# Prompt tile routed ahead of the other tiles' output projection, modulation rows by DMA, output weights read during the attention

## The reference

```python
def trunk_layer(x, cvec, p, layer, ctx, rope):
    sh1, sc1, gt1, sh2, sc2, gt2 = modulation(cvec, p['w_mod'], p['b_mod'])   # silu(c) @ w_mod + b_mod, split in 6
    h = rms_norm(x, p['g_norm1']) * (1 + sc1) + sh1
    mix, ctx_out = token_mixers(h, p, layer, ctx, rope)      # three attentions, concatenated, then @ w_out
    x = x + gt1 * mix
    h = rms_norm(x, p['g_norm2']) * (1 + sc2) + sh2
    x = x + gt2 * peer_ffn(h, p['w_pq'], p['peer_keys'], p['peer_u'], p['peer_v'])
    return x, ctx_out

def peer_ffn(h, w_pq, peer_keys, peer_u, peer_v):            # 8 heads, 128 x 128 experts, 16 chosen per head
    q = (t @ w_pq).reshape(n, PEER_HEADS, 2, PEER_DQ // 2)
    sub = jnp.einsum('nhpd,hpkd->nhpk', q, peer_keys)
    sc, ix = lax.top_k(sub, PEER_TOPK)
    cand = sc[:, :, 0, :, None] + sc[:, :, 1, None, :]       # 256 candidates a head
    best, pos = lax.top_k(cand, PEER_TOPK)
    experts = jnp.take_along_axis(cand_ix, pos, axis=-1)
    gates = softmax(best)
    act = gelu(einsum('nd,nhkd->nhk', t, peer_u[experts]))   # one gathered row of 1024 per token and expert
    return einsum('nhk,nhkd->nd', gates * act, peer_v[experts])
```

## Time and profile before

| | us |
|---|---|
| median of 3 runs | 5324.46 (5318.93 to 5358.44) |
| the profiled execution | 5334.77 |
| its span, first to last instruction | 5333.0 |

### The profile page before, as it was taken

How to read it: one execution, slowest core, us unless ns; L and a number is a source line. 1 busy time by engine, 2 the same in 40 slices (tenths; PEclk the granted TensorE clock), 3 DMA queues, 4 the chain that set the end, 5 groups by cost and what they waited for, 6 DMA issues and landing times. The chain is left out here.

```text
span 5333.0 us, 51151 instructions
## 1 busy us (share of the span) xinstructions
PE 4446.2 (83%) x15092; PEld 2252.2 (42%) x15092; DVE 3367.1 (63%) x8542; ACT 1394.3 (26%) x3530; POOL 2773.5 (52%) x2690
## 2 busy tenths in 40 slices
PE   7999898788878878777699998987988788887775
PEld 4588664333323323222256885643333233332222
DVE  5556564666676666766465655646666666766664
ACT  1211452222222222222212125422222222222221
POOL 0122000677777777777601220007777777777775
PEclk9988899899999999999999988899999999999999
DMA  7000001999999999999970000029999999999998
GB/s 263 27 3 1 16 1 68 363 409 409 409 399 406 408 404 397 400 401 397 355 251 1 3 1 16 1 96 399 409 409 409 401 401 406 400 401 393 401 390 314
DMA packets 425564, 1471.61 MB, mean 276 GB/s; under 512 B 46528, under 2 KB 52288, under 8 KB 424768
## 3 DMA queue, kind: packets, MB, share of 16 engines
q0 software_dynamic: 368640, 1342.34, 63.8%
q1 hardware_dynamic: 56640, 125.89, 6.6%
HBM read 1464.49 MB, written 3.57 MB: 275 GB/s over the span
## 5 line engine op out<-in xcount | busy, mean ns | idle before, releaser
L1601 PE MATMUL psall<-ring,diag 128*128 128x512 f32 x5120 | 2482.8, 614 | 672.2 <-DMA ring<-in_peer_v,eidx 554.0
L1413 DVE CUSTOM_DVE_ANT_0 ring<-ring,mixed 128x1024 f32<-128x1024 f32 x1280 | 1565.5, 1223 | 1010.3 <-DMA ring<-in_peer_u,eidx 1010.2
L1332 POOL DMA_INDIRECT ring<-in_peer_u,eidx x1280 | 1294.5, 1011 | 1152.4 <-DVE eidx L1270 762.4
L1601 PEld LDWEIGHTS psall<-ring,diag 128*128 128x128 f32 x5120 | 889.1, 190 | 2221.5 <-DMA ring<-in_peer_v,eidx 1468.4
L1332 POOL DMA_INDIRECT ring<-in_peer_v,eidx x1280 | 1303.8, 1019 | 408.3 <-issue 261.9
L1498 ACT ACTIVATE act<-dot 128x2 f32<-128x2 f32 x640 | 130.1, 203 | 2265.4 <-DVE dot L1413 2265.4
L1490 ACT ACTIVATE diag<-cons,wgt 128x128 f32<-128x128 f32 x1280 | 443.0, 393 | 209.6 <-DVE wgt L1393 207.6
L493 POOL TENSOR_TENSOR mlt<-lt,lmask 128x512 f32<-128x512 f32 x120 | 173.1, 1452 | 518.5 <-DVE lt L591 359.6
L1557 PE MATMUL psall<-h2T,wq 128*128 128x128 f32 (+1 forms) x1024 | 285.6, 434 | 1.3 <-DVE x L1375 1.3
L1557 PEld LDWEIGHTS psall<-h2T,wq 128*128 128x128 f32 x1024 | 157.3, 191 | 132.0 <-issue 130.2
L485 POOL MEMSET state<- 64x512 f32 x2 | 1.0, 518 | 392.2 <-POOLq L396 392.2
(11 more groups left out here) (291 smaller groups left out, 4918.8 us busy)
## 6 DMA issues: line engine op xcount, KB each, us to landing
wlate<-in_w_mod SPq DMA_DIRECT2D x32, 1024.0 KB, 5.3
wq<-in_w_pq SPq DMA_DIRECT2D x64, 512.0 KB, 6.8
ring<-in_peer_u,eidx POOLq DMA_INDIRECT x1280, 10.5
ring<-in_peer_v,eidx POOLq DMA_INDIRECT x1280, 10.5
w<-in_w_mod SPq DMA_DIRECT2D x4, 2048.0 KB, 11.2
wtm<-in_w_mod SPq DMA_DIRECT2D x4, 2048.0 KB, 18.6
wtm<-in_w_in_tm SPq DMA_DIRECT2D x4, 2048.0 KB, 9.6
ring<-in_w_out SPq DMA_DIRECT2D x4, 2048.0 KB, 11.2
```

The costliest lines, as they stand in the source:

```text
L1332: nc.gpsimd.indirect_dma_start(out=ring[:, n % slots, :], out_offset=None, in_=d[table], in_offset=bass.IndirectOffsetOnAxis(ap=p.eidx[:, ...
L1413: nc.vector.tensor_tensor_reduce(out=p.u[:, n % UR, :], in0=p.u[:, n % UR, :], in1=p.mixed[:, t, :], scale=1.0, scalar=0.0, op0=ALU.mult, ...
L1601: mm = nc.tensor.matmul(bank, p.diag[:, n % VR, :], p.v[:, n % VR, 512 * c:512 * c + 512], start=(s == 0), stop=(s == UNIT - 1))
```

## The change

- **Modulation.** The bias rows are loaded (`bias`) and added in the first step of each late chunk's sum. The sum over partitions becomes one product for each conditioning vector that leaves a row of 512 in one partition; ScalarE copies it to `mrow` and, after each pair, issues a store of the two rows to a DRAM tensor `mid_rows`. It waits for the store before its next late copy, and for all eight at the block's end. The final two steps on VectorE go.
- **Preparation.** The 22 copies of keys and values move from ScalarE to VectorE.
- **Attention.** The output weights are issued on SP's queue at the attention's start, into `u`, the tile of the u slots, which is now a tile of its own that stands from there on.
- **Tail.** The spreads go. Seven broadcasts (`gt1` x 2, `sc2` x 2, `g_norm2`, `sh2` x 2) are issued on SP's queue ahead of the keys; two more (`gt2`) after the eighth query weight. VectorE forms `(1 + sc2) * g_norm2` first. TensorE turns the prompt's h2 and makes its first queries and scores after two tiles' projections; VectorE does the steps of head 0's routing between the other tiles' residuals and norms. GpSimd waits for `h2_ready` of all tiles before the first gather of `peer_v` only.

```diff
@@ mod_and_project, SP, at each late chunk's first half
+                            sp.wait_ge(sem("bias_zero"), 1)
+                            sp.dma_start(p.bias[0:1, i % 2, :], d["b_late"][bass.ds(lay, 1), i]).then_inc(sem(f"load_bias{i % 2}"), 16)
@@ ScalarE
+                if kind == "late" and i >= 1 and a == 0:
+                    act.wait_ge(sem("row_store"), 16 * i)
                 dst, src = proj_evac(p, j, kind, i, a, b)
                 nc.scalar.activation(dst, src, ACT.Copy).then_inc(sem("proj_out"), 1)
+                if kind == "late" and a == 1:
+                    act.wait_ge(sem("proj_out"), j + 1)
+                    nc.scalar.dma_start(d["mid_rows"][i // 2:i // 2 + 1, :, WCH * (i % 2):WCH * (i % 2) + WCH],
+                                        p.mrow[0:1, :, :]).then_inc(sem("row_store"), 16)
+            act.wait_ge(sem("row_store"), 16 * LATE)
@@ VectorE
-                            late.mark(nc.vector.tensor_scalar(acc, w_late[:, k, :], p.sc[:, k, g:g + 1], None, ALU.mult))
+                            late.mark(nc.vector.scalar_tensor_tensor(out=acc, in0=w_late[:, k, :], scalar=p.sc[:, k, g:g + 1],
+                                                                     in1=p.bias[:, i % 2, :], op0=ALU.mult, op1=ALU.add))
...
@@ TensorE
-                    for blk in range(4):
-                        for g in range(2):
-                            last = nc.tensor.matmul(bank[:, 2 * blk + g:2 * blk + g + 1], sums_late[:, i % 3, g, blk * P:(blk + 1) * P],
-                                                    p.ones[:, 0:1], start=True, stop=True)
-                    last.then_inc(sem("proj"), 1)
+                    nc.tensor.matmul(bank[0:1, :], p.ones[:, 0:1], sums_late[:, i % 3, a, :], start=True, stop=True).then_inc(sem("proj"), 1)
...
@@ attend
+        @block.sync
+        def _(sp):
+            for c in range(2):
+                sp.dma_start(p.wout[:, c, :, :], d["w_out"][bass.ds(lay, 1), :, :, WCH * c:WCH * c + WCH].rearrange("l p k n -> p (l k) n")
+                             ).then_inc(sem(f"load_wout{c}"), 16)
@@ tail, SP
+            for g in range(2):
+                spread(sp, p.rows[:, 0, g, :], d["mid_rows"][0][g:g + 1, :], "load_gt1")
+            for g in range(2):
+                spread(sp, p.rows[:, 1, g, :], d["mid_rows"][2][g:g + 1, :], "load_sc2")
+            spread(sp, p.g2row, d["g_norm2"][bass.ds(lay, 1)], "load_sc2")
+            for g in range(2):
+                spread(sp, p.rows[:, 2, g, :], d["mid_rows"][1][g:g + 1, :], "load_sh2")
@@ GpSimd
             pool.wait_ge(sem("wout_mm"), 2 * NT)
-            pool.wait_ge(sem("h2_ready"), NT)
...
+                    if m == 0:
+                        pool.wait_ge(sem("h2_ready"), NT)
@@ VectorE
+            residual(0)
+            norm(0)
+            residual(1)
+            norm(1)
+            top.mark(nc.vector.memset(p.r_gs[:, :], 0.0))
+            pieces(0, 0, 6)
+            residual(2)
+            pieces(0, 6, 10)
+            norm(2)
+            residual(3)
+            pieces(0, 10, 14)
+            norm(3)
+            residual(4)
+            pieces(0, 14, TOPK)
+            norm(4)
             dve.wait_ge(sem("h2_ready"), NT)
...
+            pieces(1, 0, TOPK)
@@ ScalarE
             square(0)
+            turned(0)
             square(1)
...
+            for j in early[0:5]:
                 evacuate(j)
+            square(2)
+            square(3)
+            top_gates(p, act, 0)
+            square(4)
+            turned(1)
+            for j in early[5:9]:
                 evacuate(j)
+            turned(2)
+            evacuate(early[9])
+            turned(3)
+            turned(4)
+            top_gates(p, act, 1)
@@ TensorE
             project(0)
             project(1)
+            turn(0)
+            for j in early[0:5]:
+                step(j)
             for t in range(2, NT):
                 project(t)
+            turn(1)
             pe.wait_ge(sem("res1"), 2 * NT)
+            for j in early[5:9]:
                 step(j)
+            turn(2)
+            step(early[9])
+            turn(3)
+            turn(4)
```

More of the change, by code:

```diff
@@ L173, in mod_and_project @@
             if blk >= 1:
-                jobs.append(("late", None, blk - 1, 0, 0))
+                jobs += [("late", None, blk - 1, g, 0) for g in range(2)]
     for t in range(NT):
@@ L177, in mod_and_project @@
         if t % 2 == 0:
-            jobs.append(("late", None, 5 + t // 2, 0, 0))
+            jobs += [("late", None, 5 + t // 2, g, 0) for g in range(2)]
     jobs_until = {job[1]: j + 1 for j, job in enumerate(jobs)}
@@ L848, in prepare_attention, with copied @@
     at = {job: j for j, job in enumerate(jobs)}
+    on_vector = [job[0] in ("kn", "v") for job in jobs]
+    def copied(eng, j):
+        if on_vector[j]:
+            eng.wait_ge(sem("p_evd"), sum(on_vector[:j + 1]))
+        else:
+            eng.wait_ge(sem("p_ev"), j + 1 - sum(on_vector[:j + 1]))
     with nc.Block() as block:
@@ L918, in _ @@
                                                accum_out=p.lam[:, i:i + 1]).then_inc(sem("lam_dot"), 1)
+            for j, (kind, t, half) in enumerate(jobs):
+                if not on_vector[j]:
+                    continue
+                dve.wait_ge(sem("p_mm"), j + 1)
+                b = ps[j % 8]
+                if kind == "kn":
+                    lo, hi = (0, 512) if half == 0 else (512, KEYS)
+                    nc.vector.tensor_copy(p.kTb[0:64, t, lo:hi], b[0:64, 0:hi - lo]).then_inc(sem("p_evd"), 1)
+                else:
+                    nc.vector.tensor_copy(p.vb[:, t, :], b[:, :]).then_inc(sem("p_evd"), 1)
             for t in range(1, NT):
-                dve.wait_ge(sem("p_ev"), at[("uq", t, 1)] + 1)
+                copied(dve, at[("uq", t, 1)])
                 x = p.qb[:, t % 2, :].rearrange("p (h c) -> p h c", c=96)[:, :, 64:96]
@@ L1290, in tail, with spread @@
     nc, d, sem, ps = p.nc, p.d, p.sem, p.ps
-    vecs = [p.mod[:, 16:24, :], p.A2[:, :, :], p.mod[:, 24:32, :], p.mod[:, 40:48, :]]
-    spreads = [(v, g, half) for v in range(4) for g in range(2) for half in range(2)]
     steps, before_row = routing_steps()
-    def row_of(v, g):
-        return p.gt2[:, g, :] if v == 3 else p.rows[:, v, g, :]
+    def spread(sp, tile, row, done):
+        sp.dma_start(tile, row.to_broadcast([P, D])).then_inc(sem(done), 16)
     def block_of(g, c, b):
@@ L1321, in _ @@
                              ).then_inc(sem(f"load_q{i % WR}"), 16)
+                if i == 7:
+                    for g in range(2):
+                        spread(sp, p.gt2[:, g, :], d["mid_rows"][3][g:g + 1, :], "load_gt2")
             for name in p.front_sems:
@@ L1366, in norm, with residual @@
                 nc.vector.tensor_tensor(p.mixed[:, t, :], p.mixed[:, t, :], p.rows[:, 2, g, :], ALU.add).then_inc(sem("h2_ready"), 1)
-            for t in range(NT):
+            def residual(t):
                 g = 0 if t == 0 else 1
@@ L1431, in _ @@
                                      ps[t % 2].rearrange("p (k n) -> p k n", k=4), ACT.Copy).then_inc(sem("m_out"), 1)
-            for u, (v, g, half) in enumerate(spreads):
-                act.wait_ge(sem("row_mm"), u + 1)
-                nc.scalar.activation(row_of(v, g)[:, half * 512:half * 512 + 512], ps[2 + u % 2], ACT.Copy).then_inc(sem("row_out"), 1)
             def square(t):
@@ L1492, in _ @@
             j = len(early)
-            act.wait_ge(sem("row_mm"), len(spreads))
             for q in range(ROWS // 2):
@@ L1516, in _ @@
                 last.then_inc(sem("m_turned"), 1)
-            for u in range(len(spreads)):
-                pe.wait_ge(sem("diag2"), u + 1)
-                if u >= 2:
-                    pe.wait_ge(sem("row_out"), u - 1)
-                nc.tensor.matmul(ps[2 + u % 2][:, :], p.ones, p.diag4[:, u % 2, :], start=True, stop=True).then_inc(sem("row_mm"), 1)
             pe.wait_ge(sem("m_out"), NT)
```

122 lines of the change are left out of this document (51 added, 71 removed).

## The result

The changed kernel took 5289.15 us (median of 8 runs, 5285.57 to 5307.93) against 5329.06 us before (median of 8, 5318.93 to 5358.44): ratio 0.9923, 95% interval 0.9907 to 0.994, a gain of 32 to 50 us. The profiled execution took 5288.71 us, its span 5286.9, which is 46.1 less than the 5333.0 of before.

A forecast was written before the change was run, and what follows sets the result against it. DMA transfers bound the expert loop, which could only begin earlier: 24.9 less 3.1 less 2.1 is 19.7 us a layer, 39.4 for two, giving 5295.4 from the profiled 5334.77, scaled by 0.9981 to 5285 us; range 5264 to 5308.

The forecast's parts named there:

- Timeline of the tail: Attention's end to first gather: step times in the new order, first gather at 89.5 us against 114.4, 24.9 earlier per layer.
- Spreads and early weights: Tail's start: spreads' 14.7 us of TensorE go, broadcasts stay hidden, early read keeps output weights from being uncovered.
- First dot: Expert loop's start: first dot on a gathered row about 104 us after the stage's start, 19.1 earlier than 123.1.
- That the first gather carries its 24.9 us into the loop: Loop's start: twelve gathers last 16 us until the first dot, so nothing is lost; upper bound of loss 5.8 us.
- the rival of the first dot: Loop's start: the first dot, not the first gather, starts the loop; gain 13.9 us a layer, 5297 us; chance 0.12.
- Modulation: Modulation stage: added bias steps cost 3.1 us and the store at its end 2.1 us more per layer.
- six times 0.52: Modulation stage: VectorE's two-tensor first steps cost 0.52 us in each of six chunks, 3.1 us a layer.
- the lower bound: Modulation stage: only the sixth chunk's own two steps cost, 0.5 us, the rest absorbed by waits for transfers.
- The store's term: Modulation stage's end: copy, row store and wait for its landing cost 2.1 us more than before; bound 4.8.
- Preparation: Preparation of the attention: 22 copies moved from ScalarE to VectorE stay under TensorE; nothing gained, nothing lost.
- TensorE's clock: Tail's projection: without the spreads it runs at 1.2 GHz; throughout, 69 us more and 5422 us; chance 0.04.
- the rival in which little is lost in modulation: Modulation and loop start: little lost, loop fills faster; gain 23.3 us a layer, 5278 us; chance 0.11.

The follow-up runs named there:

- e1: Changed kernel with the tail's old order again (all five tiles projected before the prompt's queries, scores and routing): 5310.76 us, ratio 0.9955.
- e2: Changed kernel with the output weights' early read undone, issued at the tail's start ahead of the broadcast rows: 5301.62 us, ratio 0.9942.
- e8: Changed kernel with the seven broadcast rows issued behind the routing keys and first four query weights: 5294.01 us, ratio 0.9927.
- e9: Changed kernel with query weights 4 to 7 in other tiles, so 8 to 11 are read behind the prompt's first queries: 5284.31 us, ratio 0.9906.
- e6: Changed kernel with head 1's routing moved from ahead of the first dot to behind the first eight dots: 5283.36 us, ratio 0.9917.
- e3: Changed kernel without the late modulation chunks' bias: rows not loaded, first step one-tensor again; another choice of experts: 5276.94 us.
- e5: Changed kernel with GpSimd's wait for all normed rows back before the first gather, instead of before the second table's: 5293.21 us, ratio 0.993.
- e10: Changed kernel with the late modulation bias added by GpSimd to the copied row, each row stored one chunk later: 5281.6 us, ratio 0.99.
- e11: Changed kernel with query weights ahead, bias on GpSimd, head 1's routing among first dots, last two routing steps before last residual: 5291.27 us, ratio 0.9915.

## Why the prediction was right, and where it was not

The forecast of 5285 us lay 4 us under the median, its gain (39.4 for the profiled execution) at the measured 39.9; the profiled execution itself gained 46.1. The steps one by one:

- **Timeline of the tail: right to the half microsecond.** Forecast and measured (first layer, from 840.66): first product 5.0 and 4.9; turning the prompt's h2 32.5 and 32.5; queries done 42.1 and 42.2; projections done 84.8 and 85.0; row numbers done 88.5 and 88.4; first gather 89.5 and 89.3.
- **Spreads and early weights: right.** e1 confirms the split, e2 that the weights would have been uncovered (by 4.3 us), e8 that the broadcasts are hidden.
- **First dot: 104 forecast, 103.1 measured.** ScalarE's table loads stood where expected, each at the 1.28 us of the earlier trace rows:

```profile
928.28 1.28 ACT L1493 ACT_TABLE_LOAD   x1
```

- **That the first gather carries its 24.9 us into the loop: nearly.** 25.0 and 25.8 at the first gather, 23.1 and 22.5 at the 200th. The reason given (twelve gathers last until the dot) held: in the first layer no gather waits for the dot, in the second the ninth row buffer is waited for 0.67 us (0.30 is the issue). But it was too simple. It took the loop to be short of transfers from its start on, where for some 32 us GpSimd's issuing sets the pace (e9). And it missed a transfer that the earlier gather collides with: 2 MB of query weights that used to land before it. They cost some 2 us at the 200th gather and not 5.1, because they filled a sag that the old start had. e9 shows this; the rival of the first dot would have given 20 at the 200th gather, which e6 speaks against as well.
- **Modulation: wrong.** Forecast 5.2 us a layer, measured 1.5 (mean of 14 stages against the two of before; 0.9 and 1.4 in the profile shown). The failing step is "six times 0.52", which lies above the middle of its bounds because "the chunks run back to back for VectorE most of the time". They don't: VectorE waited 10.6 us for weights, as the earlier trace rows show, and most of the added steps went into those waits. TensorE reached the sixth chunk 0.9 us later (mean 70.3 against 69.3): the lower bound, that chunk's own two steps and 0.4 more. The store's term was 2.1, measured 1.5 (2.80 against 1.29). And TensorE's way from the sixth chunk to the last was 0.9 shorter (mean 30.3 against 31.2), which was not forecast: behind the wait for that chunk the granted clock fell less far on average (e3). 0.9 + 1.5 - 0.9 is 1.5. With two stages before, and 14 that scatter over 4.2 us, that 1.5 is known to about 1 us.
- **Preparation: right**, 51.4 and 52.1 before, 51.5 and 51.4 after.
- **TensorE's clock: the rival did not happen.** The granted clock was 1.00 (2.4 GHz) from the first projection on (845.60 to 854.20), after 0.71 in the transposes. In single tails of e5, e10 and e11 the low level reached into the projection and cost 2.4 to 2.5 us (last section).

So in the stretches that were changed the gain fell between the forecast and the rival in which little is lost in modulation: per layer 22.8 - 1.5, some 21 us, where 19.7 and 23.3 were expected. Two terms were off in opposite directions, the modulation 3.7 too dear, the earlier start 2.1 too good, and partly cancel. The agreement of the total to 4 us is in good part luck, since unchanged stages moved by as much.

Open: why in e3 the third chunk's weights land 1.2 us sooner than in the kernel before, with the same order of issues and the same steps; and why GpSimd's gathers take longer while the loop starts. No run tells either.

## What to carry to other kernels

Price an added step on an engine that waits for transfers at nothing until the waits ahead of it are used up; sum the engine's idle time by what ended it before multiplying a step's cost by its count. When a stage is made to start earlier, list the transfers that used to end before it: they now run beside it. When transfers sag, look first whether their issuer ever waits: one that issues back to back can itself be the limit. And before an edit of a few microseconds is measured by total time, find a mark in the trace and measure how well it repeats (here the 200th gather, within 1.3 us over six unchanged tails).

## What the hardware showed besides

**GpSimd stops VectorE even with one partition.** In e10 VectorE's two-tensor steps took 888 ns on average instead of 742 in a chunk with GpSimd's additions; its one-tensor steps never met an addition, so nothing is known of them. The Trainium skill (SBUF — State Buffer, section "SBUF: two separate sides") says that between a VectorE operation with two inputs in SBUF and a GpSimd operation that reads SBUF, whichever starts first holds a shared port pair for its whole instruction, and the other blocks fully. The trace agrees: in that chunk the two VectorE steps that met an addition took 1.76 and 1.75 us, the additions 1.27 and 1.70. For this kernel the rule alone would have spoken against e10.

**Unchanged stages move in steps with the granted clock.** DeltaNet and attention of e10 and e11, first layers, same code:

```profile
197.34:565.86 368.52, 334.38 (x2252) 287.31 (x2252) 216.76 (x370) 74.77 (x130) 87.53 (x63) 0.92 0.01 2
617.35:823.08 205.73, 185.27 (x1044) 128.85 (x1045) 146.00 (x424) 103.70 (x272) 0.00 (x0) 0.95 0.06 21
```

```profile
198.41:580.90 382.49, 347.84 (x2253) 299.73 (x2253) 216.74 (x370) 74.68 (x130) 87.47 (x63) 0.88 0.01 2
```

Fourteen microseconds of DeltaNet go with a clock of 0.92 or 0.88 while VectorE and ScalarE are busy for the same time; attention takes 205.7 at 0.95 and 212.2 at 0.91. After the short attention the tail of e10 began at 0.50 (1.2 GHz), against 0.71 in the changed kernel's:

```profile
823.08:828.46 5.38, 4.69 (x21) 3.69 (x21) 0.00 (x0) 2.99 (x5) 0.00 (x0) 0.50 0.78 278
```

Its first four product records took 3.78 us instead of 1.99, and its first gather came 2.5 us later. The second tail of e5 and the first of e11, also behind an attention of 205.7 us, began at 0.50 in the same way. Differences of this size between two single executions say nothing about a change.
